# A three-mixer encoder block on one core: the attention transposes issued with fp32r operands instead of fp32 ones, with a comparison of the two forms fed into the result

## The reference, cut to what matters

```python
h = _rmsnorm(x, norm_mix_g[l])
proj = h @ w_in[l]
...
lam = jnp.exp(jnp.sum(lp[0] * lp[1])) - jnp.exp(jnp.sum(lp[2] * lp[3])) + lam_init
# A, differential attention: 4 heads of 2 maps, chunk-causal, T5 bias
p = jax.nn.softmax(s, axis=-1)
a = p[:, :, 0] - lam * p[:, :, 1]
o_a = jnp.einsum("bhqk,bkhe->bqhe", a, v)
# B, 8 heads over own + 8 previous chunks; C, 8 heads, causal, with a cumulative log-forget bias
p = jax.nn.softmax(s, axis=-1)
o = jnp.einsum("bhqk,bkhd->bqhd", p, v)
...
x = x + (g0 * (o_a @ w_br_a) + g1 * (o_b @ w_br_b) + g2 * (o_c @ w_br_c)) @ w_out
x = x + (silu(gt) * up) @ w_down
```

## Time and profile before

| | us |
|---|---|
| median of 3 runs (lowest to highest) | 1825.85 (1825.77 to 1826.04) |
| the profiled execution, its own time | 1826.7 |
| span of its trace | 1824.9 |

### The profile page before, as it was taken

One profiled execution on the slowest core, in us unless ns is written; L12 is line 12 of the kernel. 1 busy time (PEld: TensorE's weight loads), 2 busy tenths in 40 slices (PEclk: granted clock), 3 DMA queues, 4 the chain that ended last, 5 costly groups with the idle time before them and its releaser, 6 DMA issues. The chain is left out here.

```text
span 1824.9 us, 26104 instructions
## 1 busy us (share of the span) xinstructions
PE 1805.9 (99%) x9048; PEld 1519.5 (83%) x9048; DVE 1252.2 (69%) x2374; ACT 898.3 (49%) x1742; POOL 358.1 (20%) x350
## 2 busy tenths in 40 slices
PE   8999999999999999999999999999999999999998
PEld 6888888888888888888888888888888888888886
DVE  5467766667667766677655778787776877766675
ACT  5555655667666766653424224552333333344445
POOL 2356332112111121014220000002323232200011
PEclk9999999999999999999999999999999999999999
DMA  8526333222432234244236572225656576479522
GB/s 239 157 93 196 92 95 84 61 80 58 109 93 70 59 97 124 104 133 138 98 123 218 185 257 106 104 70 196 208 195 219 170 246 220 150 254 405 196 79 92
DMA packets 195946, 268.01 MB, mean 147 GB/s; under 512 B 9989, under 2 KB 132997, under 8 KB 191865
## 3 DMA queue, kind: packets, MB, share of 16 engines
q1 hardware_dynamic: 191944, 262.07, 43.6%
q0 software_dynamic: 1664, 4.19, 1.5%
q10 hardware_dynamic: 2224, 0.30, 0.1%
HBM read 187.82 MB, written 80.02 MB: 147 GB/s over the span
## 5 line engine op out<-in xcount | busy, mean ns | idle before, releaser
L220 PE MATMUL ps<-h_hi,w_hi 128*128 128x512 f32 x888 | 361.0, 407 | 2.6 <-DVE q_stack L1062 1.2
L222 PE MATMUL ps<-h_hi,w_lo 128*128 128x512 f32 x888 | 346.9, 391 | 0.0
L221 PE MATMUL ps<-h_lo,w_hi 128*128 128x512 f32 x888 | 346.8, 391 | 0.0
L855 POOL TENSOR_TENSOR w_lo<-w_raw,w_hi 128x256 fp32r<-128x256 f32 x148 | 109.3, 770 | 470.1 <-ACT w_hi L923 470.1
L222 PEld LDWEIGHTS ps<-h_hi,w_lo 128*128 128x128 f32 x888 | 166.7, 188 | 36.8
L220 PEld LDWEIGHTS ps<-h_hi,w_hi 128*128 128x128 f32 x888 | 167.2, 188 | 35.3 <-DVE q_stack L1062 2.4
L221 PEld LDWEIGHTS ps<-h_lo,w_hi 128*128 128x128 f32 x888 | 167.4, 188 | 28.9
L1091 DVE CUSTOM_DVE_ANT_0 probs_bc<-ps,bias 128x640 f32<-128x640 f32 (+7 forms) x128 | 90.4, 707 | 75.0 <-PE ps L1247 31.6
L2288 POOL TENSOR_TENSOR bias<-w_raw 128x512 f32<-128x512 f32 x19 | 26.8, 1409 | 517.2 <-PE ps L222 327.4
L220 PE MATMUL ps<-down_ring_w,down_ring_a 128*128 128x512 f32 x308 | 119.8, 389 | 0.0
L221 PE MATMUL ps<-down_ring_w,down_ring_a 128*128 128x512 f32 x308 | 119.8, 389 | 0.0
(11 more groups left out here) (367 smaller groups left out, 4435.1 us busy)
## 6 DMA issues: line engine op xcount, KB each, us to landing
w_raw<-in_w_in SPq DMA_DIRECT2D x50, 512.0 KB, 5.4
w_raw<-in_w_gate_up SPq DMA_DIRECT2D x44, 512.0 KB, 4.2
k_stack<-k_stack SPq DMA_DIRECT2D x24, 512.0 KB, 5.4
gate_in<-gates_scratch SPq DMA_DIRECT2D x24, 512.0 KB, 3.7
down_rows<-in_w_down SPq DMA_DIRECT2D x11, 1024.0 KB, 7.1
hidden_scratch<-hidden_stage SPq DMA_DIRECT2D x22, 512.0 KB, 4.8
weight_sums_scratch<-weight_sums SPq DMA_DIRECT2D x11, 1024.0 KB, 4.9
gates_scratch<-gate_sigmoid SPq DMA_DIRECT2D x21, 512.0 KB, 2.6
```

Of the source, the lines that this page charges most:

```text
L220: nc.tensor.matmul(out, w_hi, x_hi, start=first, stop=False)
L221: nc.tensor.matmul(out, w_hi, x_lo, start=False, stop=False)
L222: return nc.tensor.matmul(out, w_lo, x_hi, start=False, stop=last)
L855: last = nc.gpsimd.tensor_tensor(w_lo[part], w_raw[part], w_hi[part].bitcast(F32), ALU.subtract)
```

## The change

The tiles that hold the probabilities and V get second names of type fp32r at the same addresses (`probs_words`, `v_words`); the transposes of `turn_v` and `turn_probs` read those with `ident_r` as fp32r and write to PSUM through an fp32r view. The readers of the PSUM banks are unchanged, and so are all waits. The other transposes (in `block_norm`, L1962, L2950) stay fp32. Near the end of `block_norm` TensorE turns one block of x as fp32 and once more as fp32r, and four instructions of DVE take the difference, multiply it by 1e9 and add its first column to `neg_lam`, the factor of mixer A's second map.

```diff
+        x_words = nc.alloc_sbuf_tensor_at("x_words", [P, TT, D], F32R, offset=113152)
+        turn_gap = sb("turn_gap", [P, TT * C_HEADS])
...
-        FORGET_BANK, C_BANK = 6, 4
+        FORGET_BANK, C_BANK, GAP_BANK = 6, 4, 5
...
             dve.wait_ge(c_turned, 1)
+            link(nc.vector.tensor_copy(turn_gap[:, :], bank(ps, GAP_BANK, TT * C_HEADS)))
+            link(nc.vector.tensor_tensor(turn_gap[:, :], turn_gap[:, :], bank(ps, GAP_BANK)[:, P:P + TT * C_HEADS], ALU.subtract))
+            link(nc.vector.tensor_scalar(turn_gap[:, :], turn_gap[:, :], 1.0e9, None, ALU.mult))
+            link(nc.vector.tensor_tensor(keep["neg_lam"][:, :], keep["neg_lam"][:, :], turn_gap[:, 0:1], ALU.add))
             nc.vector.tensor_copy(keep["c_col"][:, :], bank(ps, C_BANK, TT * C_HEADS)).then_inc(c_out, 1)
...
             project(1, 1, range(0, KT - 1))
+            nc.tensor.transpose(bank(ps, GAP_BANK, P), x_all[:, 7, 0:P], ident[:, :])
+            nc.tensor.transpose(bank(ps, GAP_BANK)[:, P:2 * P].bitcast(F32R), x_words[:, 7, 0:P], keep["ident_r"][:, :])
             pe.wait_ge(cum_done, 1)
...
+        probs_words = also("probs_words", [P, 4, T], F32R, 178176)
+        v_words = also("v_words", [P, T], F32R, 83968)
...
-                        last = nc.tensor.transpose(turn_bank[lc % 2][:, j * P:(j + 1) * P],
-                                                   v_fm[:, (4 * lc + j) * P:(4 * lc + j + 1) * P], ident[:, :])
+                        last = nc.tensor.transpose(turn_bank[lc % 2][:, j * P:(j + 1) * P].bitcast(F32R),
+                                                   v_words[:, (4 * lc + j) * P:(4 * lc + j + 1) * P], keep["ident_r"][:, :])
...
-                    src = probs_a[:, 2 * (i % 2), :]
+                    src = probs_words[:, 2 * (i % 2), :]
...
-                    src = probs_of(b, s)
+                    src = probs_words[:, s % 3, :]
...
-                        last = nc.tensor.transpose(turn_bank[lc % 2][:, x * P:(x + 1) * P],
-                                                   src[:, tile * P:(tile + 1) * P], ident[:, :])
+                        last = nc.tensor.transpose(turn_bank[lc % 2][:, x * P:(x + 1) * P].bitcast(F32R),
+                                                   src[:, tile * P:(tile + 1) * P], keep["ident_r"][:, :])
```

## The result

The changed kernel takes **1816.43 us** (median of 5 runs, 1816.18 to 1816.96) against 1825.85 (1825.61 to 1826.04) for the kernel before in the same comparison: a ratio of 0.9949 with a 95% interval of 0.9935 to 0.9963, 9.4 us less. The forecast was 1826.4, no change. The test adds nothing to `neg_lam` that shows in the output even after the factor of 1e9: in the column compared, both forms return the same words, as far as that factor shows a difference.

What follows compares the result with a forecast made beforehand. TensorE's own instruction stream was taken to bound the kernel; 0 for the transposes plus 0.55 us for the test, on the median of 1825.85, gave 1826.4 us, with 1794 to 1830 as the range for 8 in 10.

Steps and rivals of the forecast that it cites:

- What bounds the kernel: Whole kernel and attention: TensorE's own instruction stream sets the end, busy 1805.9 of 1824.9 us, clock granted in full.
- The fp32 transpose: Attention's 768 transposes: 110 ns each, a 55 ns load hidden under the predecessor and a 110 ns stream setting the pace.
- The fp32r transpose: Attention's transposes with the new type: a block costs 110 ns unchanged, 113 ns, or 57 to 60 ns.
- three readings: Per attention block: same operation, 110 ns; load-bound like an fp32r matmul, 113 ns; stream halved with quick load, 57 to 60.
- the first: Attention's transposes: the type changes only the label, 110 ns stays, 0 us; chance 44%.
- The second reading: Attention's transposes: load and stream as in an fp32r matmul, 113 ns, load-bound; +0.9 us, 1827.3 us with the test; 20%.
- The rival: Attention's transposes: stream halved, load stays quick, 110 to 59 ns; 30.4 us less, 1796 us, up to 1802; chance 23%.
- The sum: Whole kernel: 0 for the transposes plus 0.55 us for the test, 1826.4 us against the median.
- The test: End of the first block: two more transposes, 0.22 us, and four DVE instructions, 0.97 us, delay the next block by 0.55.
- The slower rival: Attention's transposes: fp32r load not hidden, 169 ns, 1861 us; milder, load-bound at 114 to 118 ns; together 13%.

Runs made afterwards that it cites:

- the series: The kernel before with eight series of 16 fp32 transposes, fp32r transposes or fp32r matmuls, some with 64 columns loaded or streamed, in its first block: 1839.54 us, one execution.
- experiment 4: The changed kernel without the test, with the last block of each of attention's 172 transpose groups as fp32 again: 1814.41 us, ratio 0.9938.
- experiment 5: Projection pieces moved one step later in B and C units: on the kernel before 1835.95 us; on the changed kernel without the test 1829.37 us.

## Why the prediction was wrong

**What bounds the kernel: right.** TensorE's stream set the end before and after, the clock did not move, and of 10.9 us taken from the groups 10.2 arrived at the end of attention. Without the test, medians show 9.8 (1825.64 to 1815.88).

**The fp32 transpose: right.** "A quick load (55 ns, hidden under its predecessor) and a stream that takes the whole 110 ns" is what the series show, with 109 for the stream and at most 63 for the load (of 64 rows; 60 to 67 by experiment 4's estimate).

**The fp32r transpose: the step that failed.** The prediction put it as three readings and took the first, "in a transpose the whole word has to arrive, and the quick load beside the slow stream belongs to transposing, as no fp32r matmul shows it". The series show the contrary for the stream: it belongs to the type fp32, for with fp32r it is at most 60 ns, near the 57 of the fp32r matmuls. The second reading had that stream right and its load wrong: "Fp32r words load in 112 ns" holds for the matmuls (112) and not for the transposes (84). The prediction drew this bound from fp32r matmuls, the nearest rows there were, and assumed that an fp32r load costs the same whatever instruction follows. The rival had the stream right too, and a load that stays at 57 to 60 wrong. So the truth lay between two of the readings, each of which had one of the two halves. The page "Perfetto Trace Analysis" of the Trainium skill, section "Engine Utilization", which halves the rate in the mode FP32_LOW_HIGH, agrees with the stream of 109 against at most 60, if that is the mode of an fp32 transpose, which no run shows. The price of 107 ns for loading 128 columns, from the page "TensorE: Matmul & The Clock Gate" of the Trainium skill, section "LDWEIGHTS (loading the stationary operand)", agrees with the matmul's 112 and with neither transpose (84, and at most 63), so the prediction should not have carried it over.

That 1816.4 us lies in the range given for 8 in 10 (1794 to 1830) is no credit to the working: the range was that wide to reach from one reading to the other, and no reading put a time between 1802 and 1825. A gain clear of noise had been given 0.24.

**The sum.** In the rival's form it is (768 - 172) x 51 ns = 30.4 us; with the measured distance it is (768 - 172) x 26 = 15.5 us. Of these, 4.6 did not arrive: what the groups cost above their ideal pace, at (n - 1) x 110 ns before, (n - 1) x 84 after, and 114 for the last block in both, grew from 12.9 to 17.5 us. 15.5 - 4.6 = 10.9. Of the 4.6, 1.2 is seen in the waits, as in experiment 5: that of L220 for `q_stack` rose from 1.2 to 2.4 us in the kernel after. Ahead of the groups, by starts, the time grew by no more than 0.35 us in sum; of the waits there, that for `probs_a` fell from 1.9 to 0.8 us and that for `probs_bc` rose from 0.8 to 1.1:

```profile
PE ps L220 <- DVE q_stack L1072: 2.4, 7, 0.4
PE ps L1283 <- ACT probs_bc L975: 1.1, 1, 1.1
```

A second part is inside the groups. It is plainest at those of one block: behind a matmul of 128 columns, whose stream is 57 ns, a load of 84 ns cannot hide, 27 ns more, whereas the fp32 load of at most 63 nearly can. The 12 blocks that stand so lost 17 to 25 ns each, the 8 behind 256 or 384 columns (113 ns and more) lost nothing, and with fp32 at the last block all 12 are back where they were (124 where they had been 124). So the cause is shown for single blocks; they make up some 0.25 us. That the first or last block of longer groups pays in the same way is likely, as fp32 at the last block took 18 to 24 ns off these too, but the other 3 us of the 4.6 were not told apart. The prediction's second reading had the groups' last blocks gaining 8 ns each, and the 12 single ones lost 17 to 25.

**The test: right.** +0.55 forecast, +0.51 in the traces, 0.55 and 0.69 by runs; and it was right that the meeting is counted from DVE's end. The places in time came out earlier: the copy to `c_col` starts at 56.84 and the next block at 57.51, where 57.4 and 58.0 were given, since the first block of that execution was ahead by some 0.5 us before it came to the test.

**The slower rival (169 ns, or 114 to 118): did not occur.** The load runs under the transpose before it, as every fp32r load does.

**What stays open.** Why 128 columns of fp32r words load in 84 ns ahead of a transpose and in 112 ahead of a matmul, and fp32 words in at most 63, no run here shows; only the three numbers are measured. The matmuls of the series also load another tile (`w_hi`) than the transposes (`x_words`), and that the instruction and not the tile makes the difference was not tested by itself. What part of V's gain alone reaches the end was not settled either.

## What to carry to other kernels

Where transposes stand on the engine that sets the end, the type is a price of its own: on this kernel fp32r names for the same words took an fp32 transpose of 128 x 128 from 109 to 84 ns, and fp32 for the last block before an fp32r matmul took 17 to 24 ns more off each group. A price for a form that the trace lacks must be taken apart into load and stream, and each half bracketed by itself: the truth may take one half from one neighbour and the other half from a place that no neighbour shows, and a range from the cheapest pair to the dearest says so. Work that was placed as cover keeps its place when what it follows gets faster, even if a wait now stands ahead of it: moving it cost 10.2 and 13.5 us. And a form that needs a constant of its own type may put its maker on the path: the wait for `ident_r` took back what the 32 transposes of x had won.

## What the runs showed that had not been expected

- Weight loads differ by what they feed, with 128 columns each: at most 63 ns for an fp32 transpose, 84 for an fp32r transpose, 112 for an fp32r matmul.
- The profile's load records hide this: 140 and 139 ns for the two transposes, 190 for the matmul. Record lengths rank the forms only in part, while the distances between starts in a series with half the load or half the stream separate them.
- An fp32 transpose streams its 128 columns in 109 ns, about two clocks per column at 2.4 GHz, and an fp32r one in at most 60, one clock per column.
- Single blocks behind a matmul of 128 columns became slower (124 to 142 ns behind the mask), those behind 256 or 384 columns did not, and all longer groups became faster.
- The granted clock fell to 0.50 in two stretches of the changed kernel with the pieces moved, each behind a wait of 1.58 us, and that was 3 of the 13.5 us lost. It fell once in the kernel with the series too, from 69.6 to 73.0 us, behind an idle time of 0.45 us at the meeting of the engines, where no other kernel here shows it.
